# Working off the cache pages in fours instead of pairs, behind every second weight block

## What is computed

```python
def token_mixing(x, fox_cache, page_table, conv_buf, S0, mix):
    h = rmsnorm(x, g_pre)
    qa, ka, va, logf, qg, kg, vg, g, beta, z, gate_a, gate_b, new_buf = mixer_inputs(h, ...)   # h @ w_in
    ...
    o_a = fox_sample(qa, ka, va, logf, cache_k, cache_v, cache_logf, page_table)   # the 8 sample tokens
    ...

def fox_sample(q, k, v, logf, cache_k, cache_v, cache_logf, page_table):
    past_k = cache_k[page_table].reshape(DB, -1, FOX_HEADS, FOX_HEAD_DIM)
    past_v = cache_v[page_table].reshape(DB, -1, FOX_HEADS, FOX_HEAD_DIM)
    ...
    return fox_block(q, c[:, P:], P + jnp.arange(T), k_all, v_all, c, jnp.arange(P + T))
```

## Time and profile before

| | before |
|---|---|
| time, median of 3 runs | 1687.4 us (1685.17 to 1690.0) |
| the profiled execution, its own time | 1685.08 us |
| its span, first to last instruction | 1683.2 us |
| mean granted TensorE clock | 0.965 |
| TensorE matmul busy | 1574.1 us, 94% of the span |
| VectorE, ScalarE, GpSimd busy | 601.4, 502.1, 131.7 us |
| moved by DMA | 268.51 MB, mean 160 GB/s over the span |

### The profile page before, as it was taken

One profiled execution on the slowest core, in us unless ns is written; L12 is line 12 of the kernel. 1 busy time (PEld: TensorE's weight loads), 2 busy tenths in 40 slices (PEclk: granted clock), 3 DMA queues, 4 the chain that ended last, 5 costly groups with the idle time before them and its releaser, 6 DMA issues. The chain is left out here.

```text
span 1683.2 us, 31105 instructions
## 1 busy us (share of the span) xinstructions
PE 1574.1 (94%) x12650; PEld 1407.5 (84%) x12650; DVE 601.4 (36%) x889; ACT 502.1 (30%) x742; POOL 131.7 (8%) x152
## 2 busy tenths in 40 slices
PE   5999998999688999999999999978988999998995
PEld 4999998999577888877856776658978999998995
DVE  3333333121633654132455432335434333332113
ACT  4223222221521355221233223232343322222221
POOL 0000000000152000332100220011000000000000
PEclk8999999999899999999979999998999999999998
DMA  3222223222359978999965456745302222222221
GB/s 105 91 97 87 88 99 106 69 86 76 96 172 376 335 267 298 356 332 361 354 225 192 162 188 212 232 164 165 108 31 88 87 87 95 92 92 86 86 86 51
DMA packets 111866, 268.51 MB, mean 160 GB/s; under 512 B 15389, under 2 KB 15902, under 8 KB 111018
## 3 DMA queue, kind: packets, MB, share of 16 engines
q1 hardware_dynamic: 105514, 244.01, 42.3%
q0 software_dynamic: 6272, 23.34, 3.8%
HBM read 253.04 MB, written 14.26 MB: 159 GB/s over the span
## 5 line engine op out<-in xcount | busy, mean ns | idle before, releaser
L130 DVE TENSOR_TENSOR w_low<-w_raw,w_high 128x1024 fp32r<-128x1024 f32 (+1 forms) x180 | 233.0, 1296 | 766.9 <-ACT w_high L126 766.9
L126 ACT ACTIVATE w_high<-w_raw 128x1024 fp32r<-128x1024 f32 (+1 forms) x180 | 200.6, 1116 | 755.5 <-PE psum L151 726.7
L147 PE MATMUL psum<-h_high,w_high 128*128 128x260 f32 x1408 | 286.0, 284 | 16.4 <-DVE h_low L227 16.4
L151 PE MATMUL psum<-h_high,w_low 128*128 128x260 f32 x1408 | 284.9, 284 | 0.0
L149 PE MATMUL psum<-h_low,w_high 128*128 128x260 f32 x1408 | 284.5, 284 | 0.0
L147 PEld LDWEIGHTS psum<-h_high,w_high 128*128 128x128 f32 x1408 | 218.1, 190 | 18.8 <-issue 14.5
L151 PEld LDWEIGHTS psum<-h_high,w_low 128*128 128x128 f32 x1408 | 218.3, 189 | 0.0
L149 PEld LDWEIGHTS psum<-h_low,w_high 128*128 128x128 f32 x1408 | 217.6, 189 | 0.0
L147 PE MATMUL psum<-a_high,w_high 128*128 128x260 f32 x704 | 146.4, 289 | 10.4 <-DVE a_low L383 10.4
L147 PE MATMUL psum<-mix_h_high,w_high 128*128 128x260 f32 x704 | 147.5, 291 | 6.9 <-DVE mix_h_low L227 6.9
L149 PE MATMUL psum<-a_low,w_high 128*128 128x260 f32 x704 | 143.1, 285 | 0.0
(11 more groups left out here) (300 smaller groups left out, 1795.8 us busy)
## 6 DMA issues: line engine op xcount, KB each, us to landing
kv_ring<-in_cache_k SPq DMA_DIRECT2D x256, 256.0 KB, 4.0
kv_ring<-in_cache_v SPq DMA_DIRECT2D x256, 256.0 KB, 3.9
w_raw<-in_w_gu SPq DMA_DIRECT2D x88, 512.0 KB, 3.3
w_raw<-in_w_dn SPq DMA_DIRECT2D x32, 704.0 KB, 4.1
w_raw<-in_w_proj SPq DMA_DIRECT2D x44, 512.0 KB, 6.6
spill<-h_f POOLq DMA_DIRECT2D x20, 260.0 KB, 5.0
gates<-spill POOLq DMA_DIRECT2D x16, 260.0 KB, 3.5
w_raw<-in_w_merge SPq DMA_DIRECT2D x8, 512.0 KB, 4.5
```

The source lines that it names most:

```text
L126: act.activation(w_high[:, u, 0:nk, :], w_raw[:, u, 0:nk, :], ACT.Copy).then_inc(high_done, 1)
L130: dve.tensor_tensor(w_low[:, u, 0:nk, :], w_raw[:, u, 0:nk, :], w_high[:, u, 0:nk, :].bitcast(F32), ALU.subtract).then_inc(low_done, 1)
L147: pe.matmul(out[h], w_high[:, u, k, :], high[:, k0 + j, tok[h]], start=s, stop=False)
L151: mm = pe.matmul(out[h], w_low[:, u, k, :], high[:, k0 + j, tok[h]], start=False, stop=e)
```

## The change

In three places of TensorE's loop the pair behind an even block is held back and worked off with the next one, behind the odd block. The same 38 pairs run in the same order with the same operations; only 19 of them move by one block. No other engine's program is changed, SyncE's neither.

```diff
-                        if KEY0 <= n < KEY0 + 2 * NG:
+                        if KEY0 <= n < KEY0 + 2 * NG and (n - KEY0) % 2:
+                            key_pair(0, n - KEY0 - 1)
                             key_pair(0, n - KEY0)
...
-                        if VAL0 <= n < VAL0 + 2 * NG:
+                        if VAL0 <= n < VAL0 + 2 * NG and (n - VAL0) % 2:
+                            value_pair(0, n - VAL0 - 1)
                             value_pair(0, n - VAL0)
...
-                        if n >= KEY1:
+                        if n >= KEY1 and (n - KEY1) % 2:
+                            key_pair(1, n - KEY1 - 1)
                             key_pair(1, n - KEY1)
```

## The result

The change made the kernel slower: 1697.7 us, median of 4 runs (1693.65 to 1698.32), against 1687.63 for the kernel before (4 runs, 1685.17 to 1690.0), a ratio of 1.0055 with a 95% interval of 1.0033 to 1.0076. The prediction was 1687.2 in a range of 1678 to 1695, so both the time and the range missed; slower had the least chance of the three. The profiled execution after took 1693.65 us, its span is 1691.8, 8.6 more than before.

The account below looks back on a forecast made before the run. TensorE, busy for 94% of the span, sets the pace, with DMA close behind. Gains of 2.9 and 5 less 7.7 give 0.2 us off 1685.08, so 1684.9; with 2.3 for the median 1687.2, range 1678 to 1695.

Parts of the forecast that it names:

- Term 1, the borders: Moved pairs from block 10 on lose a border of up to 0.31 us each: 2.9 gained, from 1 to 4.5.
- Term 2, the start: Blocks 4 to 10: block 5 fills the wait for queries; 5 us gained, bounds 3 to 8.
- The mechanism of K(5): Key pair 5: SyncE's pages move at 0.206 MB/us beside GpSimd's transfers, so TensorE stands for 9 us before it.
- Term 3, pages that come late: Second pairs of a turn, key stage to round 1, wait for pages: 7.7 us lost, from 0.5 to 17.5.
- Key stage: Blocks 13 and 17: pages take 15.4 us where TensorE returns after 15.3; 0.5 lost, from 0 to 3.
- n = 25: Block 25: value pair 3's pages come late beside the `o_proj` store; 3.5 us lost, from 0 to 7.
- n = 37: Block 37: pages come late with `o_state_s` in the way; 1 us lost, from 0 to 2.
- n = 41: Block 41: second `o_state_s` falls into the wait of round 1's key pair 3; 2.2 us lost, 0.5 to 4.
- K(6) of round 1: Behind the projection, key pair 6 waits for a slot freed one block later: 0.5 us lost, 0 to 1.5.
- Slower: the burst makes DMA the bound: Every second pair waits, clock falls above about 3 us: 1696; page waits after block 10 pass 13 us; chance 0.18.
- The ring holds: Pages come at 0.387 or better throughout, late pages cost 2, start keeps 7, borders 3: 1679 us; chance 0.24.
- Nothing stays of the start: Key pair 5's pages come no earlier than 543.93, the start gains 1: 4 us slower, 1691; chance 0.12.

Follow-up runs that it names:

- e6: The changed kernel with half of each page fetched after the ring's first filling: 1678.63 us, ratio 0.9947 to the kernel before.
- e1: The whole change run once more for a second profile: ratio 1.0053 to the kernel before.
- e2: The kernel before with only round 0's key pairs in fours, values and round 1 as before: ratio 0.9977.
- e16: The whole change with the `o_proj` store cut to an eighth and the `o_state_s` stores to a sixteenth: ratio 1.0005 to the kernel before.
- e13: The kernel before with only the first key pair moved, from behind block 4 to behind block 5: 1677.38 us, ratio 0.9969.
- e9: The kernel before with GpSimd's `x_spill` and `state_in` issued behind block 17 instead of block 6: ratio 0.9958.
- e14: The kernel before with only the first key pair moved, and `x_spill` and `state_in` issued behind block 19: 1668.39 us, ratio 0.9915.
- e12: The kernel before with only value pairs in fours, `o_proj` store cut to an eighth, sample state stores to a sixteenth: ratio 1.0007.
- e7: The changed kernel with SyncE asking for each weight block ahead of the pages in its half turn: ratio 1.0095 to the kernel before.
- e8: The kernel before with only value pairs in fours, and VectorE making `new_spread` ahead of the split of block 26: ratio 1.0049.
- e5: The kernel before with half of each page fetched after the ring's first filling: 1686.31 us, ratio 0.9977.
- e11: The kernel before with round 0's keys and values of blocks 26 to 35 in fours, `x_spill` and `state_in` behind block 17: ratio 1.0003.
- e10: The kernel before with round 0's key pairs in fours, and `x_spill` and `state_in` issued behind block 17: ratio 0.9982.

## Why the prediction was wrong

By its own steps:

**Term 1, the borders: right.** 2.9 predicted. e6 shows 1.1 for the five moved value pairs from 26 to 36, 0.3 at 23, 0.1 at 37, 0.5 in round 1, and 0.32 for each turn of two blocks and two key pairs of round 0. About 3.7 in all. My 0.31 for a whole border and the second pair's 1.73 to 1.76 hold. The Trainium skill (TensorEngine Tiling (Array Packing), Key Properties) says that a change of the tiling mode drains TensorE. By that rule a pair in four column strips between blocks on the whole array should cost more than its matmuls, and the traces agree, with 0.3 us a pair; it fits, but no run here separates the drain from other costs of a border.

**Term 2, the start: right.** 5 predicted, 4.4 measured at P(10) and 4.5 at P(12). P(5) follows at once, the queries cost 1.31, P(8) started at 519.8 where 515.5 was predicted, of which the 2.3 at P(4) and the 1.36 before K(3) are the most; the stand before K(5) is 7.47 and its pair takes 3.64. The place isn't fixed: in e1 the long wait, 5.29 us, stands before K(3) and K(5) waits 1.96, with 5.1 gained at P(12). So the size was right, and the place in most profiles (e2, e6 and e16 have it before K(5) too). What I didn't see is that this term belongs to one pair (e13), the other 18 having no part in it.

**The mechanism of K(5): right.** SyncE's pages are slow beside GpSimd's large transfers: 0.206 MB/us against 0.388 in all, about half. e9 and e14, which move these transfers, make the waits go. The Trainium skill (DMA: Bandwidth & Descriptors, Queues, rings and completion order) says that each DMA engine goes round between the queue rows that have work. By that rule two busy queues with packets of one size would share about evenly, and the trace agrees, with 0.206 of 0.388.

**Term 3, pages that come late: this step failed.** I put it at 7.7 lost, with bounds of 0.5 and 17.5. In the profile after, the stretch from P(12) to the end lost 10.9, and with the borders' gain of about 3 taken off the term is 14; in e1 it is 18. Added up by place it is 16, for the rest behind P(42) ran at a higher clock than in the profile of before (0.84 against 0.79 from 840 to 905). By place, from the profile after (e1 in brackets where it differs):

- Key stage, 0.5 predicted. 2.7 lost from 12 to 20, with waits of 1.15 and 2.42 and the borders' 1.3 eaten up: 4.0. I had compared 15.3 with 15.4 us and called it even. It was even, and where it is even each disturbance becomes a wait.
- n = 25, 3.5 predicted. 1.8 (3.9). The place and the cause, `o_proj`, were right (e12). The wait that TensorE shows is another: for VectorE, held by weight block 26.
- n = 37, 1 predicted. 3.9 (5.2): a wait of 2.59 and 1.5 more because the clock fell behind it. I had priced no clock there.
- n = 41, 2.2 predicted. 4.7: mostly 2.46 for VectorE's `sample_o`, 0.67 for pages, and 1.8 for the tail of the lower clock in P(38), against the borders' 0.5.
- K(6) of round 1, 0.5 predicted: 1.84.

So the size was off by about 6 to 10 us, with the right stores at the right places. Two costs are missing from it. The first is the price of the clock: I took it at 1 at one place of five. The second is the weight blocks. Each `load_block` stands behind a burst of pages in SyncE's order, so that ScalarE and VectorE stand in their splits, with small operations behind them that TensorE needs. I had named late weight blocks as a way to be wrong altogether, and gave it no price. It is not the sole cause, though: e7 and e8 take it away and only uncover the pages.

**The sum and the median.** 10.5 us lie between 1687.2 and 1697.7. From P(12) on 5.8 are missing (10.9 lost where the terms give 2.6 - 7.7 = -5.1), up to P(12) 0.8 (4.5 where they give 5.3), 2.3 is the stall ahead of P(4), and 1.7 is that the median lies 4.0 above the profiled execution where before it was 2.3. That is the 10.5, to rounding. Two small slips stand in the working: the stand before K(5), written as 9, is 9.6 by its own terms, and the 1.5 of the rule beside it is 1.4. Neither enters the sum. The stall is no part of the change, and e1, whose profile is without it, has a ratio of 1.0053 all the same.

**The rivals.** "Slower: the burst makes DMA the bound" came nearest, with 1696 for 1697.7. Its own mark, more than 13 us of page waits after n = 10, wasn't reached: 6.6 us for keys and 2.6 for values, plus 4.2 for VectorE behind late blocks. That its time fits is in part luck, since 4.0 of it are the stall and the distance of the median from the profile. "The ring holds" is refuted by these waits. e6 shows what that case would be, 5 to 8 us faster than e5 where I had worked out 8, but only with half of the bytes. "Nothing stays of the start" is refuted by the table.

## What to carry over

A ring without spare slots is fed at the rhythm in which it is emptied: taking steps in fours halves the borders, but first idles the DMA and then wants everything at once, and whatever shares the queue (here the weight blocks and, through the engines' program order, small copies) becomes late too. Ask for each moved piece what it gains by itself: here one of 19 brought the gain, and the others together cost more than their borders were worth. Where two waits stand before the same work, taking away one shows the other, so look at which transfer makes both late; moving `x_spill` and `state_in` behind block 19 was worth 9 us beside the 5 of the best order of the pairs.

## What was not expected of the hardware

**Stalls of issue.** In some executions TensorE stands for 0.3 to 1.1 us at a time in blocks 1 to 3 while it waits for nothing that the profile shows. P(1) to P(4) then take up to 30.5 us instead of 23.0, which makes most of the column "to P4". From e11:

```profile
473.98 0.53 PE L1483 MATMUL psum<-mix_h_high,w_small_low 128*96 128x260 f32 x1 [1.12 <-issue]
...
476.80 0.38 PE L1483 MATMUL psum<-mix_h_high,w_small_low 128*96 128x260 f32 x1 [1.02 <-issue]
```

They stand between 465 and 480 us, just behind the filling of the ring at 364 to 371 GB/s. In e11 such waits add up to 4.5 us, and the clock falls behind them (0.50 from 475 to 480). It isn't the kernel that decides: the eight experiments from e5 to e12 ran on one chip, on two occasions, and all eight profiles have the stall, of 1.8 to 7.5 us, e5 and e9 with the order of before among them. The other eight, on two other chips, have none, with a filling just as fast (e1: 375 to 382 GB/s). The chip, or what ran beside it, goes with the stall; what starts it wasn't tried. (Of the profile after, which has 3.5 us of it, the chip isn't known.) The times of before go the same way, with medians of 1689.0 and 1685.5 on that chip against 1683.0 and 1682.8 on the others. So ratios within one chip can be compared here, and profiles from different chips only from P(4) on.

**How little waiting moves the clock.** After waits of 1.0 to 2.0 us in the projection the clock held in all profiles; after 2.04 and 2.19 (e11), 2.15 (e1), 2.59 and 2.97 us (e9) it had fallen, and the work behind took 1.6 to 2.3 us longer, after the 2.59 us 3.3. After 2.42, 2.85 (e10) and 3.40 us (e14) it had not. So the length of the wait alone doesn't tell it, and the 3 us above which my rival had the clock fall were too many.
